# Splitting four feed-forward weight pieces ahead and halving the projection's tail around a turn

## What is computed

```python
x_mixed = x + gt1 * merge_branches(hx, [y_pool, y_sgu, y_lru, y_na], w_branch[l], w_gate[l], w_out[l])
...
hx2 = modulate(rms_norm(x_mixed, g_ffn[l]), sh2, sc2)
x = x_mixed + gt2 * swiglu(hx2, w_ffn_gate[l], w_ffn_up[l], w_ffn_down[l])
return rms_norm(x, g_final)
```

## Time and profile before

| | us |
|---|---|
| median of 3 runs | 1635.61 (1634.35 to 1636.22) |
| the profiled execution, its own time | 1635.51 |
| its span, first to last instruction | 1633.8 |
| TensorE busy | 1603.9 |
| VectorE busy | 1103.1 |
| ScalarE busy | 730.8 |

### The profile page before, as it was taken

The page is one execution under the profiler, slowest core; times in us unless marked ns, Lnnn a source line. Parts: engine busy times, 40 slices in busy tenths (PEclk is TensorE's granted clock), DMA queues, the critical chain, the costliest instruction groups (busy, mean ns, idle before and its releaser), DMA issues.

```text
span 1633.8 us, 22715 instructions
## 1 busy us (share of the span) xinstructions
PE 1603.9 (98%) x7899; PEld 1322.8 (81%) x7899; DVE 1103.1 (68%) x1271; ACT 730.8 (45%) x820; POOL 159.6 (10%) x296
## 2 busy tenths in 40 slices
PE   6999999999999999999999999999999999999998
PEld 4678798987788888888887888888888888888886
DVE  4333556878888888877896576867755556456577
ACT  5333234468744444444445544443444444434444
POOL 1002111000022122123020010101100000000000
PEclk9999999999999999999999999999999999999999
DMA  9998746645589889899685677878776666666654
GB/s 346 356 357 245 243 144 203 222 147 156 187 298 326 282 297 337 278 340 341 220 287 164 179 235 244 280 233 268 248 254 193 191 193 187 188 191 191 190 174 139
DMA packets 200545, 390.28 MB, mean 239 GB/s; under 512 B 14400, under 2 KB 47408, under 8 KB 199584
## 3 DMA queue, kind: packets, MB, share of 16 engines
q1 hardware_dynamic: 176960, 312.51, 59.7%
q0 software_dynamic: 23312, 76.79, 14.1%
q10 hardware_dynamic: 208, 0.11, 0.0%
HBM read 386.35 MB, written 3.01 MB: 238 GB/s over the span
## 4 chain that ended last, share of the span: by engine, by line
PE 90%; DMA 5%; DVE 2%; issue 1%; ACT 1%; SPq 0%; POOL 0%; POOLq 0%; DVEq 0%; ACTq 0%
PE ps L1439 24%; PE ps L1441 24%; PE ps L1440 24%; PE ps L1411 5%; PE ps L1412 4%; PE ps L1413 4%; DMA BR<-in_w_mod 4%; PE ps L1407 2%; PE ps L1492 1%; DVE BR L915 1%; DMA MR<-in_w_mod 1%; DVE LO L803 1%; PE ps L1603 0%; PE ps L1590 0%; PE ps L1629 0%
## 5 line engine op out<-in xcount | busy, mean ns | idle before, releaser
L803 DVE TENSOR_TENSOR LO<-RAW,HI 128x1024 fp32r<-128x1024 f32 x519 | 633.0, 1223 | 399.5 <-ACT HI L451 398.3
L451 ACT ACTIVATE HI<-RAW 128x1024 fp32r<-128x1024 f32 x519 | 548.4, 1060 | 751.9 <-PE ps L1441 626.2
L1439 PE MATMUL ps<-HI,H 128*128 128x512 f32 x1840 | 720.6, 392 | 1.4 <-DVE ATT L1110 1.0
L1441 PE MATMUL ps<-HI,H 128*128 128x512 f32 x1840 | 716.4, 389 | 0.0
L1440 PE MATMUL ps<-LO,H 128*128 128x512 f32 x1840 | 716.0, 389 | 0.0
L1439 PEld LDWEIGHTS ps<-HI,H 128*128 128x128 f32 x1840 | 345.5, 188 | 74.5 <-DVE ATT L1110 1.4
L1441 PEld LDWEIGHTS ps<-HI,H 128*128 128x128 f32 x1840 | 345.4, 188 | 72.2
L1440 PEld LDWEIGHTS ps<-LO,H 128*128 128x128 f32 x1840 | 345.6, 188 | 72.0 <-issue 1.2
L413 POOL DMA_DIRECT2D BR<-in_w_mod x224 | 120.4, 538 | 765.2 <-DVE BR L915 306.4
L915 DVE SCALAR_TENSOR_TENSOR BR<-BR,SCF 128x512 f32<-128x512 f32 (+1 forms) x210 | 156.7, 746 | 12.7 <-DMA BR<-in_w_mod 10.8
L1411 PE MATMUL ps<-H,HI 128*128 128x256 f32 (+1 forms) x384 | 125.7, 327 | 0.1
(11 more groups left out here) (258 smaller groups left out, 759.2 us busy)
## 6 DMA issues: line engine op xcount, KB each, us to landing
RAW<-in_w_gate SPq DMA_DIRECT2D x128, 512.0 KB, 4.7
BR<-in_w_mod POOLq DMA_DIRECT2D x224, 256.0 KB, 4.6
RAW<-in_w_ffn_gate SPq DMA_DIRECT2D x88, 512.0 KB, 3.8
RAW<-in_w_ffn_up SPq DMA_DIRECT2D x88, 512.0 KB, 3.7
RAW<-in_w_ffn_down SPq DMA_DIRECT2D x88, 512.0 KB, 3.7
RAW<-in_w_in SPq DMA_DIRECT2D x64, 512.0 KB, 5.7
BR<-in_w_mod SPq DMA_DIRECT2D x50, 512.0 KB, 9.4
RAW<-in_w_branch SPq DMA_DIRECT2D x32, 512.0 KB, 5.2
```

Of the source, the lines that this page charges most:

```text
L451: act.activation(HI[:, j % RING, :], RAW[:, j % RING, :], ACT.Copy).then_inc(hi_done, 1)
L803: tt(LO[:, j % RING, :], RAW[:, j % RING, :], HI[:, j % RING, :], ALU.subtract).then_inc(lo_done, 1)
L1439: mm(o, xh, wh, start=first and t == 0, stop=False, skip_group_check=True)
L1441: i = mm(o, xl, wh, start=False, stop=last and t == 1, skip_group_check=True)
```

## The change

Four things change.

- **Ahead pieces.** The first four feed-forward pieces are split not into the HI and LO ring but into rows 8 to 15 and 2 to 7, 0, 1 of H[:, 0] (AHEAD_HI, AHEAD_LO), so their splits wait for their transfer and no longer for a ring slot. TensorE reads them from there.
- **Gate sums** of group 0 move to rows 0 to 5 of H[:, 0]; the fourth reuses the first's rows, and waits for the spread that read them.
- **The tail.** The last projection group does pieces 0 to 3 for both halves and pieces 4 to 7 in two passes; turn 0 stands in the second pass between pieces 6 and 7.
- **The lists** of ScalarE and VectorE are rewritten: all four ahead splits first; pieces 4 to 7 (`high_behind`) with waits for projection pieces 4 to 7; then units 8 to 11 and pieces 8 to 11 in turn.

```diff
--- before.py
+++ after.py
@@ -151,8 +151,11 @@
         Y = H[:, 0, :, :, :]
         HID = H[:, 0, 0:G4, :, :]
         HIDL = H[:, 0, G4:2 * G4, :, :]
-        SUMS_HI = [[H[:, 0, 8 * g + n, :, :].rearrange("p l t -> p (l t)") for n in range(4)] for g in range(2)]
-        SUMS_LO = [[H[:, 0, 8 * g + 4 + n, :, :].rearrange("p l t -> p (l t)") for n in range(4)] for g in range(2)]
+        ROWS = [H[:, 0, k, :, :].rearrange("p l t -> p (l t)") for k in range(KT)]
+        SUMS_HI = [[ROWS[2 * (n % 3)] for n in range(4)], ROWS[8:12]]
+        SUMS_LO = [[ROWS[2 * (n % 3) + 1] for n in range(4)], ROWS[12:16]]
+        AHEAD = [H[:, 0, k:k + 2, :, :].rearrange("p k l t -> p (k l t)") for k in (8, 10, 12, 14, 2, 4, 6, 0)]
+        AHEAD_HI, AHEAD_LO = AHEAD[0::2], AHEAD[1::2]
         SCF = sb("SCF", [P, 2, KT])
         CST = sb("CST", [P, CST_N])
         IDENT = CST[:, 0:P]
@@ -685,6 +688,8 @@
             def sums_high(g, n, src, groups):
 
                 act.wait_ge(s("mod_used"), groups * KT + 2)
+                if g == 0 and n == 3:
+                    act.wait_ge(s("gate1_spread"), 1)
                 act.activation(SUMS_HI[g][n], src, ACT.Copy).then_inc(s("sums_hi"), 1)
 
             for n in range(4):
@@ -720,25 +725,42 @@
                 act.wait_ge(s("h2_odd"), u + 1)
                 act.activation(HX[:, k:k + 2, 0, tokens], HF[:, k:k + 2, tokens], ACT.Copy).then_inc(s("h2_hi"), 1)
 
-            high(FFN0 // 4, 0)
-            high(FFN0 // 4, 1)
+            def high_ahead(w):
+
+                act.wait_ge(landed[w], FFN0 // 4 * 16 + 16)
+                if w == 2:
+                    act.wait_ge(s("gate1_spread"), 1)
+                act.activation(AHEAD_HI[w], RAW[:, w, :], ACT.Copy).then_inc(hi_done, 1)
+
+            def high_behind(w):
+
+                act.wait_ge(landed[w % RING], FFN0 // 4 * 16 + 32)
+                act.wait_ge(used, FFN0 + w - 3)
+                act.activation(HI[:, w % RING, :], RAW[:, w % RING, :], ACT.Copy).then_inc(hi_done, 1)
+
+            for w in range(4):
+                high_ahead(w)
             act.activation(ST[:, 62:63], EPSC[:, 0:1], ACT.Sqrt)
             square_last(0)
             root(0)
-            high(FFN0 // 4, 2)
+            high_behind(4)
             act.wait_ge(s("a2"), 1)
             h2_high(0)
             h2_high(1)
-            high(FFN0 // 4, 3)
+            square_last(1)
             h2_high(2)
-            square_last(1)
+            root(1)
             h2_high(3)
-            root(1)
+            high_behind(5)
             h2_high(4)
             h2_high(5)
-            for w in range(4, 10):
-                high(FFN0 // 4, w)
-                h2_high(w + 2)
+            high_behind(6)
+            h2_high(6)
+            high_behind(7)
+            h2_high(7)
+            for u in range(8, 12):
+                h2_high(u)
+                high(FFN0 // 4, u)
 
             def ffn_gate(m, last):
                 act.wait_ge(used, last + 1 + 4)
@@ -750,10 +772,9 @@
                 act.wait_ge(s("hid_turned"), m + 1)
                 act.activation(hid[:, :, 0, :], pair(2).rearrange("p b (k t) -> p (b k) t", k=2), ACT.Copy).then_inc(s("hid_hi"), 1)
 
-            for w in range(10, 16):
+            ffn_gate(0, FFN0 + 7)
+            for w in range(12, 16):
                 high(FFN0 // 4, w)
-                if w == 11:
-                    ffn_gate(0, FFN0 + 7)
             with act.Fori(1, FC - 1) as m:
                 base = LOOP0 - 24 + m * 24
                 for w in range(24):
@@ -1162,6 +1183,8 @@
                 stt(A2[:, :], MC2[:, KT:2 * KT], 1.0, PA[:, PA_GFFN:PA_GFFN + KT], ALU.add, ALU.mult).then_inc(s("a2"), 1)
 
             def sums_low(g, n, src):
+                if g == 0 and n == 3:
+                    dve.wait_ge(s("gate1_spread"), 1)
                 split_low("sums_hi", 4 * g + n + 1, SUMS_LO[g][n], src, SUMS_HI[g][n], "sums_lo")
 
             def gate1_row(n):
@@ -1240,33 +1263,43 @@
                 split_low("h2_hi", u + 1, HX[:, 2 * q:2 * q + 2, 1, tokens], HF[:, 2 * q:2 * q + 2, tokens],
                           HX[:, 2 * q:2 * q + 2, 0, tokens], "h2_lo")
 
-            low(FFN0, 0)
-            low(FFN0 + 1, 1)
+            def low_ahead(w):
+                dve.wait_ge(hi_done, FFN0 + w + 1)
+                if w >= 2:
+                    dve.wait_ge(s("gate1_spread"), w - 1)
+                tt(AHEAD_LO[w], RAW[:, w, :], AHEAD_HI[w], ALU.subtract).then_inc(lo_done, 1)
+
+            low_ahead(0)
+            low_ahead(1)
             last_scaled(0)
             last_added(0)
+            low_ahead(2)
             squares_summed(0)
             rstd_diagonal(0)
+            low_ahead(3)
             h2_odd(0)
             h2_odd(1)
             h2_low(0)
-            h2_odd(2)
             h2_low(1)
-            low(FFN0 + 2, 2)
             last_scaled(1)
             last_added(1)
+            h2_odd(2)
+            h2_odd(3)
             h2_low(2)
-            h2_odd(3)
-            low(FFN0 + 3, 3)
             squares_summed(1)
             h2_low(3)
             rstd_diagonal(1)
-            for u in (4, 5):
+            low(FFN0 + 4, 4)
+            low(FFN0 + 5, 5)
+            for u in (4, 5, 6, 7):
                 h2_odd(u)
                 h2_low(u)
-            for w in range(4, 10):
-                h2_odd(w + 2)
-                low(FFN0 + w, w)
-                h2_low(w + 2)
+                if u >= 6:
+                    low(FFN0 + u, u)
+            for u in range(8, 12):
+                h2_odd(u)
+                h2_low(u)
+                low(FFN0 + u, u)
 
             def ffn_gated(m):
                 dve.wait_ge(s("ffn_sig"), m + 1)
@@ -1775,11 +1808,11 @@
                     i = spread(0, n)
                 i.then_inc(s("gate1_spread"), 1)
 
-            def row_pass(p, j, lhs, q, o, k0, first, last):
+            def row_pass(p, hi, lo, lhs, q, o, k0, first, last):
 
                 ready(p)
                 for t in range(2):
-                    wh, wl = HI[:, j % RING, t * BW:(t + 1) * BW], LO[:, j % RING, t * BW:(t + 1) * BW]
+                    wh, wl = hi[:, t * BW:(t + 1) * BW], lo[:, t * BW:(t + 1) * BW]
                     xh, xl = lhs(k0 + t, q)
                     i = rows3(o, xh, xl, wh, wl, first and t == 0, last and t == 1)
                 if q:
@@ -1810,7 +1843,7 @@
                     pe.wait_ge(s("merge_read"), 15 + n)
                 else:
                     pe.wait_ge(s("xm_new"), n - 1)
-                for j in range(8 if n < 3 else 6):
+                for j in range(8 if n < 3 else 4):
                     if n == 0 and j % 2 == 0:
                         pe.wait_ge(s("mg_lo"), j // 2 + 1)
                     piece_rows(OUT0 + 8 * n + j, j, tokens_of(HX), row_banks(2 * (n % 2)), 2 * j, j == 0, j == 7)
@@ -1822,17 +1855,19 @@
                     if 8 * n + j == 26:
                         gate1_spread(3, 1)
             for q in range(2):
-                for j in (6, 7):
-                    i = row_pass(OUT0 + 24 + j, j, tokens_of(HX), q, ps[:, 2 + q, :], 2 * j, False, j == 7)
+                for j in range(4, 8):
+                    i = row_pass(OUT0 + 24 + j, HI[:, j % RING, :], LO[:, j % RING, :], tokens_of(HX), q, ps[:, 2 + q, :],
+                                 2 * j, False, j == 7)
+                    if q and j == 6:
+                        h2_turn(0)
                 if q == 0:
                     i.then_inc(s("out_half"), 1)
 
-            h2_turn(0)
             h2_turn(1)
             for q in range(2):
                 for w in range(4):
                     pe.wait_ge(s("h2_lo"), 4 * q + w + 1)
-                    row_pass(FFN0 + w, w, tokens_of(HX), q, ps[:, q, :], 2 * w, w == 0, False)
+                    row_pass(FFN0 + w, AHEAD_HI[w], AHEAD_LO[w], tokens_of(HX), q, ps[:, q, :], 2 * w, w == 0, False)
                     if q and w == 1:
                         h2_turn(4)
                 if q == 0:
```

## The result

The change takes 1656.2 us (1654.6 to 1657.9, four runs) where the kernel before takes 1635.9 in the same comparison (1634.4 to 1637.9): a ratio of 1.0124, 95% interval 1.0112 to 1.0136. It is slower, as forecast, but by 20.3 us and not by 14.7; the time lies above the range. The profiled execution is the fastest of the four, 1654.6, and what follows is read from it; the other three took 1.0 to 3.3 us longer at a mean granted clock of 0.990 to 0.991 instead of 0.992, and they have no trace.

What follows compares the result with a forecast made beforehand. TensorE, busy for 98% of the span, was taken to bound the kernel. 1635.5 - 0.95 + 13.8 - 0.6 = 1647.8; with 2.4 for the clock 1650.2 us, range 1645.0 to 1654.0.

Steps and rivals of the forecast that it cites:

- Part 1: Projection tail in half passes, leading turn inside it, four weight pieces split ahead: 0.95 us gained.
- sum of lost time: From the last projection matmul to feed-forward piece 4 in the kernel before: 4.6 us lost, six restarts of 0.11 included.
- Part 2: Order behind the tail: pieces 5, 6 and 7 each wait for piece 8, 9 or 10's split and the next unit; 13.8 us lost.
- the chain: From piece 4's last matmul through piece 8's splits and unit 9's odd row, high and low parts to TensorE: 4.73 us.
- Part 3: Granted clock falling from 2.4 to 1.2 GHz around the three new TensorE waits: 2.4 us lost in all.
- The price for each lies between 0 and 1.6 us: Clock cost of each new TensorE wait, its upper end the 1.6 us of the one early fall in the trace before.
- the 2.4 us taken: Clock cost of all three new waits, half the price for each, since a fall inside a wait is partly over.
- 1647.8: Forecast time in us without the clock's cost; also the rival that the clock never falls, chance 0.29.
- The rival in which each wait pays in full: Each of the three new TensorE waits pays the full clock price, 4.8 us in all: 1652.6 us, chance 0.17.
- The rival on the other side: Ring order behind piece 4 doesn't bind, the tail's gain stands alone: 1634.6 us, 1633.0 at the bound; chance 0.08.

Runs made afterwards that it cites:

- filled waits: The change with 16 idle 512-column matmuls in each of TensorE's waits at pieces 5, 6 and 7: 1648.0 us, ratio 1.0078 to the kernel before.
- the units first: The change with activation units 8 to 11 made before the weight splits of pieces 8 to 11: 1634.2 us, ratio 0.9993 to the kernel before.

## Why the prediction was right and where it was wrong

**Part 1, 0.95 us gained: right in size, in part by luck.** In the change itself piece 4 starts 35.43 us into the passage, before it was 36.44 (905.86 less 869.42): 1.01 gained. Six kernels below with the same code up to there have 35.25 to 36.01, a gain of 0.4 to 1.2, so that a single execution comes this close to 0.95 is luck. The single waits were shorter than forecast: the first turn starts 1.05 us late (1.2 forecast), piece 2 of the first half waits 0.60 us, 0.76 late (0.95 forecast); behind turn 3 it is 0.58, as before. The residual of the first half starts at 877.90, 2.72 us earlier in the passage, as forecast; but that is two half pieces of six matmuls, not the four that the prediction names. And its sum of lost time in the trace of before counts six restarts where the trace has five waits. Neither changes the time that it gives. The reason given for the first wait was right too: ScalarE waits 1.41 us for the fourth ahead piece's transfer, then comes the table load, then the square.

```profile
904.47 0.48 PE L1472 MATMUL ps<-HI,H 128*128 128x512 f32 x1
```
```profile
878.55 1.06 ACT L733 ACTIVATE H<-RAW 128x1024 fp32r<-128x1024 f32 x1 [1.41 <-DMA RAW<-in_w_ffn_gate]
879.63 1.28 ACT L743 ACT_TABLE_LOAD   x1
...
881.03 0.62 ACT L711 ACTIVATE ATT<-BR 128x512 f32<-128x512 f32 x1
```

**Part 2, 13.8 us: right.** 4.73 us by the chain, 4.76 measured, three times; 13.9 by the filled waits. The waits came 9.5 and 9.8 us apart, not 7.3 as forecast, because the pieces between ran at half clock; with the waits filled they are 7.4 apart. Part 2 could be foreseen from two facts, a slot counter in the code and the order of one list, with durations of four rows.

**Part 3, the clock: wrong, and this alone put the time outside the range.** The step that failed is the sentence "The price for each lies between 0 and 1.6 us", and with it the 2.4 us taken. The clock cost 7.1 us in the profiled execution. Two things in that step were wrong. The end of the range was the price of the one fall in the trace of before, and one fall seen once is no upper bound. The same early stretch, which the change doesn't touch, shows it: seven steps of its 512-column matmuls took 2.88 us in the profile of the change (33.16 to 36.04, 1.3 us over steps of 0.23), and twelve took 5.25 in that of the units first, 2.5 us over.

```profile
33.76 0.79 PE L1446 MATMUL ps<-H,HI 128*128 128x512 f32 x1
...
39.01 0.39 PE L1446 MATMUL ps<-H,HI 128*128 128x512 f32 x1
```

And the price was halved because a fall inside a wait would be partly over when work starts. It wasn't: each of the three pieces began at the lower level and ran its first ten to thirteen matmuls there. Against the same pieces with the waits filled, the three falls cost 2.1, 2.2 and 2.6 us. What the rows did offer as a price is a piece wholly at the lower level: 12 matmuls at 0.43 instead of 0.23, 2.4 us, three of them 7.2. With it the sum is 1647.8 + 7.2 = 1655.0, beside 1654.6 for the profiled execution. It is no strict bound, since the third fall ran on into piece 8. The rival in which each wait pays in full was the right mechanism at a wrong price, 4.8.

The rule of the Trainium skill, TensorE: Matmul & The Clock Gate, section Why this matters for your kernels, held: every wait of 4.4 us was followed by the lower level. Of the two waits of 2.56 us one had a fall behind it, too, and the other had none.

**The rival on the other side** (the ring order doesn't bind) is out: it binds in each kernel that has it.

## What to carry to other kernels

When a list of work for an engine is rewritten, look in it for a step that waits for the end of work X and stands ahead of a step that the work after X needs; such a pair is a full stop of the fast engine, whatever the rest gains. Price a wait of TensorE of some microseconds with the work behind it at half clock, not only with its own length: filling it with useless matmuls gave back 7 us here. And compare kernels by the stretch that the edit touches: its waits can be listed one by one, where the intervals of whole times were some 1.5 us wide to either side. But look first at how much that stretch scatters by itself, here 0.8 us.

## What was not expected of the hardware

The clock fell in two kernels while TensorE was working: 1.5 us after a wait of 2.56 us had ended, and 1.0 and 0.2 us after waits of 3.06 and 3.07 us. And behind equal waits of 4.37 us it came back after 7 matmuls in one kernel and after 11 to 13 in the change; so equal waits don't cost equal time. And the first turn's wait, in kernels with identical code up to there, was 0.74, 0.81, 0.89, 0.97, 1.07, 1.41 and 1.54 us: it follows the landing of one transfer. In all seven ScalarE's fourth ahead split, released by that landing, starts 9.35 to 10.15 us into the passage, and the turn 4.3 us behind it each time. That scatter is part of what whole times show.
